# A two-layer diffusion trunk on one core: weight splits on GpSimd, stacked fp32r offset products, and head 0 prepared beside the last recurrence units

## The chip, the cores and the metric

One NeuronCore of a Trainium2 chip runs the whole program once; the metric is the device time of that execution in microseconds. All inputs lie in HBM, and nothing is computed on the host.

## The reference

Two layers with weights of their own each. A layer takes 1152 tokens (128 context tokens and 1024 latent tokens) of width 1024:

```python
h = rmsnorm(x, norm1_g) * (1 + sc1) + sh1            # sc, sh, g: SiLU(cond) @ w_ada + b_ada
q_m, k_m, v_m, o_m, gate_m, conv_in, cq_raw, ckv_raw, krope = split_in(h @ w_in)
y_m = rmsnorm(mlstm_forward + mlstm_backward, mlstm_norm_g) * sigmoid(o_m)   # 4 heads x 64
y_c = silu(layernorm(depthwise_conv31(glu(conv_in)), ln_g, ln_b)) @ pw_w     # 256 channels
q = rmsnorm(rmsnorm(cq_raw) @ w_uq); k, v = rmsnorm_of_keys(rmsnorm(ckv_raw) @ w_ukv, krope)
y_a = softmax(rope(q) @ rope([k, k_ctx]).T / sqrt(96)) @ [v, v_ctx]          # 8 heads
x = x + g1 * (concat(y_m, y_c, y_a) @ w_out)
x = x + g2 * ((silu(gate) * up) @ ffn_w_down)        # gate, up = rmsnorm(x, norm2_g)... @ ffn_w_gu
```

The mLSTM is a matrix memory with an exponential gate, scanned forwards and backwards and stabilised by running maxima. The kernel computes it in tiles of 128 tokens: within a tile as masked scores of keys and queries, between tiles by a carried state.

## The kernel before

Each engine has one hand-written instruction stream, and counted semaphores (`x.at(l, k)`: the k-th signal of layer l) order the streams. An engine executes its own stream strictly in order, so what stands behind a waiting instruction waits too. A Python loop over the two layers writes both, with the same structure.

Products in full precision are made of rounded halves: `a_hi`, `a_lo` and `w_hi`, `w_lo` are fp32r tiles (the value rounded, and what the rounding left), and a product is `a_hi*w_hi + a_lo*w_hi + a_hi*w_lo`. `w_high(n)` (L1199, ScalarE, "ACT" in rows) makes `w_hi` of chunk n, `w_low(n)` (L1588 on VectorE, "DVE") `w_lo`. A second `w_low` on GpSimd ("POOL", L2171) serves the chunks 16 to 23 of `w_out`. Weights for chunk n are double-buffered.

A layer runs in these stages on TensorE ("PE"):

1. Chunks 0 to 12 of `w_in`, 72 matmuls of 384 columns each (`chunk3`, L692), with small work `beside` them: tiles of the gates turned, `ml_tr` and `ml_cols` handed to and fro, key rows (`kr_rows`), `decay` products for `dcol` (L792). On DVE in that time: 31 convolution taps over two channel blocks (`taps`, 62 instructions, L1684, L1686, L1688, L1689), the gate scans, and the nine `w_low(6..14)` between the taps.
2. Chunks 13 to 15 as 72 blocks `dense(first, last)` of three matmuls each (L808 to L810): 24 before the value tiles, 48 spread over the units.
3. `value_tiles` (L768) turn the values; ACT copies them to `vaug` (L1297), which lies where the convolution's input was. So that copy waits for `cv_y`, the end of the taps, and PE waits for the copy.
4. 18 units of the recurrence (`UN`; `for n in range(UN)`): `offsets(n + 2)` (L828), `memory(n)` (L849 to L856), `key_query` (L837), dense blocks and `side(n)`, which holds column sums (L865) and row spreading (L748) for the norms of the latents and of the convolution. `offsets` spreads four rows of gate offsets `rr` over all partitions with fp32 products against a selector `sel` in `mc`.
5. Preparation of attention: head 0's `proj_q` (L962) and `proj_k` (L973), the memory's norm (`hsq`, `hnum`), its turning (L927) and gating (`yt`, `a_hi`, `a_lo`), the convolution's pointwise product (`pointwise`, L941), the turned queries and keys (L980, L986), head 1's projections, 25 products for the row maxima of head 0 (L1003, reduced by DVE at L1980), and `max_rows` (L1011). In layer 0, eight `last_modulation` calls (L718, 128 matmuls of two columns) stand between them. The loads `ctxk`, `krt`, `hw`, `rope_in`, `pw` are issued by SyncE ("SP") once `w_used` has counted 16, the last dense block.
6. Attention: 8 heads of 19 steps (`GLOBAL`), starting with L1024.
7. `w_out` as chunks 16 to 23 (in layer 0, DVE computes 16 modulations beside them, L2063), then the feed-forward part (L1103, L1132).

## Time and profile before

| | |
|---|---|
| time, three runs | 3636.89, 3638.81 (median), 3642.09 us |
| profiled execution | 3644.04 us, its span 3642.2 us |
| mean granted TensorE clock | 0.950 of full speed |
| busy: PE, PEld, DVE, ACT, POOL | 3385.1 (93%), 3020.9, 1878.8 (52%), 864.7 (24%), 321.7 us (9%) |
| layer 0 / layer 1 | the same events about 1795.5 us apart |
| end of the convolution taps on DVE | 272.5 / 2068.1 us |
| PE restarts at the value tiles | 275.43 / 2070.98 us |
| last dense block done | 419.3 / 2214.8 us |
| first attention score (L1024) | 504.75 / 2290.59 us |

Starts are microseconds from the beginning of the span. The four landmarks at the foot of the table cut each layer into the stages that the change touches. The sum in the prediction is made in the profiled execution's time; that execution took 5.2 us longer than the median.

### The profile page before, as it was taken

To read this page: it belongs to the slowest core of one execution; us is meant where nothing else is said; L and a number is where in the kernel's file an instruction comes from. 1 tells how busy PE (TensorE), PEld (TensorE's weight loads), DVE (VectorE), ACT (ScalarE), POOL (GpSimd) and SP (SyncE) were. 2 spreads that over 40 slices of the span, in tenths; PEclk is the share of its full clock that TensorE was granted. 3 is DMA by queue.
4 is the path that set the end of the run, shared out by engine and by line. 5 is a ranking of instruction groups with operands and counts; after the bars stand their busy time and mean duration, and the time that the engine had idled before them with its cause. 6 is when DMAs were issued, how large, how long until landed. Compare 5 with 4: busy or idle time off the path is not lost. (4 is left out here: it accounts for less than half of the span.)

```text
span 3642.2 us, 45449 instructions
## 1 busy us (share of the span) xinstructions
PE 3385.1 (93%) x18642; PEld 3020.9 (83%) x18642; DVE 1878.8 (52%) x3068; ACT 864.7 (24%) x1332; POOL 321.7 (9%) x276
## 2 busy tenths in 40 slices
PE   5989989999899999999989896999997999999998
PEld 4988856557789999999979885655586999999998
DVE  6694644444666556565366655444415434433343
ACT  3212334444221111011132223344422111111100
POOL 0000111222110000000010001122121000000000
PEclk7996879999999999999999888899998999999999
DMA  5210100003322222122021000000110111111111
GB/s 246 88 32 1 62 4 4 3 12 122 106 75 76 86 75 81 63 83 80 28 87 45 18 3 16 2 4 3 45 66 32 50 35 46 35 46 46 46 35 53
DMA packets 44805, 185.60 MB, mean 51 GB/s; under 512 B 5440, under 2 KB 8960, under 8 KB 43136
## 3 DMA queue, kind: packets, MB, share of 16 engines
q1 hardware_dynamic: 37760, 158.58, 12.5%
q0 software_dynamic: 6912, 25.17, 2.4%
q8 instruction: 93, 1.52, 0.2%
q14 instruction: 40, 0.33, 0.0%
HBM read 169.14 MB, written 14.59 MB: 50 GB/s over the span
## 5 line engine op out<-in xcount | busy, mean ns | idle before, releaser
L1103 PE MATMUL ps<-a_hi,gu_hi 128*128 128x384 f32 x2112 | 711.9, 337 | 30.4 <-DVE a_lo L1630 24.2
L1103 PE MATMUL ps<-a_lo,gu_hi 128*128 128x384 f32 x2112 | 710.1, 336 | 0.0
L1103 PE MATMUL ps<-a_hi,gu_lo 128*128 128x384 f32 x2112 | 710.0, 336 | 0.0
L1103 PEld LDWEIGHTS ps<-a_hi,gu_hi 128*128 128x128 f32 x2112 | 400.0, 189 | 36.8 <-issue 18.0
L1103 PEld LDWEIGHTS ps<-a_lo,gu_hi 128*128 128x128 f32 x2112 | 400.1, 189 | 0.0
L1103 PEld LDWEIGHTS ps<-a_hi,gu_lo 128*128 128x128 f32 x2112 | 400.0, 189 | 0.0
L1132 PE MATMUL ps<-g_hi,d_hi 128*128 128x384 f32 x1056 | 354.3, 336 | 4.3 <-DVE g_lo L2081 4.3
L2079 DVE TENSOR_TENSOR at<-ps,sg 128x384 f32<-128x384 f32 x132 | 73.4, 556 | 545.9 <-ACT sg L1511 545.9
L1132 PE MATMUL ps<-g_lo,d_hi 128*128 128x384 f32 x1056 | 354.2, 335 | 0.0
L1132 PE MATMUL ps<-g_hi,d_lo 128*128 128x384 f32 x1056 | 353.9, 335 | 0.0
L1980 DVE TENSOR_REDUCE pmx<-ps 128x1 f32<-128x384 f32 (+1 forms) x400 | 213.4, 543 | 235.5 <-PE ps L1003 235.2
L1038 PE MATMUL ps<-pt,va 128*128 128x512 f32 (+1 forms) x608 | 306.3, 586 | 20.6 <-issue 20.6
L2095 DVE SCALAR_TENSOR_TENSOR z<-ps,mods,z 128x384 f32<-128x384 f32 x352 | 217.7, 618 | 128.0 <-PE ps L1132 128.0
L1511 ACT ACTIVATE sg<-ps 128x384 f32<-128x384 f32 x132 | 65.0, 492 | 906.7 <-PE ps L1103 906.7
L692 PE MATMUL ps<-a_hi,w_hi 128*128 128x384 f32 x1008 | 234.3, 340 | 35.0 <-DVE a_lo L1630 25.1
L1421 ACT ACTIVATE pt<-ps 128x512 f32<-128x512 f32 (+1 forms) x304 | 176.1, 579 | 321.3 <-PE ps L1026 319.4
L1003 PEld LDWEIGHTS ps<-kh,qh 96*128 96x128 f32 x400 | 79.5, 199 | 192.1 <-DVE pmx L1980 187.7
L692 PE MATMUL ps<-a_lo,w_hi 128*128 128x384 f32 x1008 | 230.0, 335 | 0.0
L692 PE MATMUL ps<-a_hi,w_lo 128*128 128x384 f32 x1008 | 229.9, 335 | 0.0
L692 PEld LDWEIGHTS ps<-a_hi,w_hi 128*128 128x128 f32 x1008 | 179.1, 189 | 47.7 <-issue 30.5
L1003 PE MATMUL ps<-kh,qh 96*128 96x384 f32 (+1 forms) x400 | 180.7, 471 | 33.3 <-DVE pmx L1980 29.5
L1132 PEld LDWEIGHTS ps<-g_hi,d_hi 128*128 128x128 f32 x1056 | 199.1, 189 | 5.0 <-DVE g_lo L2081 5.0
(261 smaller groups left out, 5095.2 us busy)
## 6 DMA issues: line engine op xcount, KB each, us to landing
f_raw<-wgu SPq DMA_DIRECT2D x88, 512.0 KB, 4.4
diag<-wada_c POOLq DMA_DIRECT2D x48, 512.0 KB, 3.8
f_raw<-wdn SPq DMA_DIRECT2D x44, 512.0 KB, 4.4
w_raw<-win SPq DMA_DIRECT2D x32, 512.0 KB, 3.6
spill<-z SPq DMA_DIRECT2D x2, 4608.0 KB
z<-spill SPq DMA_DIRECT2D x2, 4608.0 KB, 13.6
w_raw<-wout SPq DMA_DIRECT2D x16, 512.0 KB, 4.0
wada_o<-wada_b SPq DMA_DIRECT2D x16, 512.0 KB, 3.7
```

Of the source, the lines that this page charges most:

```text
L692: mm = MM(ps[:, 3 * (n % 2) + b, 0:BLK], w, a[:, k, b * BLK:(b + 1) * BLK], start=(k == 0 and first), stop=(k == KC - 1 and last))
L1003: MM(ps[:, 5 if h else u % 3, 0:keys.stop - keys.start], qh[h % 2][0:QK, t * P:(t + 1) * P], kh[h % 2][0:QK, keys], start=True, stop=True) ...
L1038: MM(ps[:, bank, 0:n], va[h % 2][:, kt], pt[:, g % 3, 0:n], start=first, stop=(kt == 0 or kt == KTILES - 1)).then_inc(at_pv.sem, 1)
L1103: mm = MM(ps[:, 2 * (v % 2) + part, 0:BLK], w, a[:, k, b * BLK:(b + 1) * BLK], start=(k == 0 and j == 0), stop=(k == KC - 1 and j == 2))
L1132: mm = MM(ps[:, 4 + n % 4, 0:BLK], w[:, f, os_], a[:, f, bs], start=(f == 0 and j == 0), stop=(f == 1 and j == 2))
L1421: A(pt[:, g % 3, 0:n], ps[:, src, 0:n], ACT.Exp, scale=SCALE_A).then_inc(at_exp.sem, 1)
L1511: A(sg[:, v % 2, :], ps[:, 2 * (v % 2), 0:BLK], ACT.Silu).then_inc(f_silu.sem, 1)
L1980: V.tensor_reduce(out, src, AX.X, ALU.max).then_inc(at_mx.sem, 1)
L2079: link(TT(at[:, v % 2, :], ps[:, 2 * (v % 2) + 1, 0:BLK], sg[:, v % 2, :], ALU.mult))
L2095: ins = STT(x[:, o, bs], ps[:, bank, 0:BLK], gate[:, 1:2], x[:, o, bs], ALU.mult, ALU.add)
```

## The change

- `offsets` becomes one product in fp32r over 128 rows instead of an fp32 product over 64: the rounded rows stand in `rrx[0:64]`, what the rounding left in `rrx[64:128]`, and the selector has a one in both halves. For that DVE casts the selector once per layer (L1700), copies `rr` (L1762) and subtracts (L1770), and ACT makes two copies of 64x1152 at chunk 9.
- `w_low(4..15)` goes from DVE to GpSimd, eleven in a row and the last inside the loop of `kw`.
- The six `side_tiles` for key rows run one chunk earlier, the 18 key transposes go inside chunk 12, the copy `dcol` goes from DVE to ACT. Of the 24 dense blocks that stood before the value tiles, 8 stay there or between them (6 before the first value tile that needs the buffers freed by ACT), and 64 are spread over units 0 to 13.
- `proj_q(0)` and `proj_k(0)` run beside units 15 and 16, and their loads are issued once `w_hi(15)` and `w_lo(15)` exist. The order of the sums, means and spreads in `side` is changed, with nine spread rows in one sequence.
- Head 0's preparation: DVE turns the keys, GpSimd the queries; the memory's turning, gating and head 1's projections stand between the maxima of head 0; `pointwise` fills the waits for the turned queries and keys; the low halves of the memory and the convolution are made by GpSimd; the maxima use two PSUM banks instead of three.
- The eight `last_modulation`s are gone from PE; DVE computes 24 modulations instead of 16 beside `w_out` of layer 0.

The core of the diff:

```diff
@@ PE
                     for h in range(HEADS_M):
-                        sel = mc[0:DH, M_SEL + (4 * d + h) * P:M_SEL + (4 * d + h + 1) * P]
-                        mm = MM(ps[:, 3, h * P:(h + 1) * P], sel, rr[:, t * P:(t + 1) * P], start=True, stop=True)
+                        mm = MM(ps[:, 3, h * P:(h + 1) * P], sel[:, (4 * d + h) * P:(4 * d + h + 1) * P], rrx[:, t * P:(t + 1) * P],
+                                start=True, stop=True)
...
-                for k in range(5):
-                    key_tiles(k, 6)
-                    dense(4 * k, 4 * k + 4)
...
                 offsets(0)
-                dense(20, 24)
+                dense(0, 4)
+                pe.wait_ge(ml_dcol.sem, ml_dcol.at(l, 1))
                 for k in range(5):
                     value_tiles(k, 6 + k % 2)
+                    if k < 4:
+                        dense(4 + k, 5 + k)
...
                 for n in range(UN):
                     memory(n)
-                    cuts = [24 + 48 * (2 * n + j) // (2 * UN) for j in range(3)]
+                    cuts = [min(72, 8 + 64 * (2 * n + j) // 28) for j in range(3)]
                     dense(cuts[0], cuts[1])
                     if n + 2 < UN:
                         offsets(n + 2)
-                    if n < 15:
-                        side(n)
+                    side(n)
                     dense(cuts[1], cuts[2])
...
+                    if n == 15:
+                        proj_q(0)
+                    if n == 16:
+                        proj_k(0)
...
-                proj_q(0)
-                last_modulation(0, 2)
-                proj_k(0)
-                last_modulation(2, 4)
-                turned_memory()
-                last_modulation(4, 6)
                 pointwise(0)
-                pe.wait_ge(at_k1.sem, at_k1.at(l, 1))
+                pointwise(1, 0, 1)
                 turn_q(0)
+                pointwise(1, 1, 2)
                 turn_k(0)
-                pointwise(1)
-                proj_q(1)
-                proj_k(1)
+                pointwise(1, 2, NB)
                 for u in range(UNITS):
+                    if u == 2:
+                        turned_memory(0)
+                    if u == 6:
+                        proj_q(1)
+                        turned_memory(1)
+                    if u == 10:
+                        proj_k(1)
                     max_unit(0, u)
+                pe.wait_ge(at_k1.sem, at_k1.at(l, 1))
                 max_rows(0)
@@ DVE
                 dve.wait_ge(z_free_d.sem, z_free_d.at(l, 2))
+                dve.wait_ge(ml_in.sem, ml_in.at(l, 32))
+                V.tensor_copy(sel[:, :], sel_in[:, :])
...
                 taps(9, 13)
-                w_low(11)
+                rows_low()
                 taps(13, 17)
-                w_low(12)
...
-                sums(0)
-                inverse(0)
+                sums(0)
+                inverse(0)
+                keys_turned()
+                hv = den[:, 0, :, :].rearrange("p t h -> p (t h)")
+                dve.wait_ge(ml_hsq.sem, ml_hsq.at(l, 1))
+                link(V.tensor_reduce(hv, hsq[:, :, :], AX.X, ALU.add))
...
                 low_q(0)
+                TT(hn[:, :, :, :], hnum[:, :, :, :], spread(den[:, 2, :, :], DH), ALU.mult).then_inc(ml_h.sem, 1)
                 low_k(0)
...
                 for un in range(UNITS):
+                    if un in (4, 8):
+                        gated_memory(un // 4 - 1)
...
-                        cut = (0, 2, 4, 7, 10, 12, 14, 16)
+                        cut = (0, 3, 6, 10, 14, 18, 21, LATE)
@@ POOL
                 low_halves(0)
+                for n in range(4, 15):
+                    w_low(n)
                 pool.wait_ge(ml_cols.sem, ml_cols.at(l, 6))
...
                 for n in range(UN):
+                    if n == 6:
+                        w_low(15)
@@ SP
+                sp.wait_ge(w_hi_ok.sem, w_hi_ok.at(l, 15))
+                sp.wait_ge(w_lo_ok.sem, w_lo_ok.at(l, 15))
+                sp.dma_start(ctxk[:, :], ctx_ckv[bass.ds(l, 1)].rearrange("a p n -> (a p) n")).then_inc(at_in.sem, 16)
...
                 sp.wait_ge(w_used.sem, w_used.at(l, 16))
```

On DVE, in the convolution of layer 0, the stream before has a weight split after every four taps or so (`x8` are four taps on two channel blocks; `krt` is a copy of key rows, `rb` the last row operation of the gates):

```order
L1739 TENSOR_TENSOR rb<-rr,mrow 64x1152
L1696 COPY krt<-ps 128x32
L1686 SCALAR_TENSOR_TENSOR yc<-u,vecs,yc 128x1182 x4
L1588 TENSOR_TENSOR w_lo<-w_raw,w_hi 128x1024
L1686 SCALAR_TENSOR_TENSOR yc<-u,vecs,yc 128x1182 x8
L1588 TENSOR_TENSOR w_lo<-w_raw,w_hi 128x1024
L1686 SCALAR_TENSOR_TENSOR yc<-u,vecs,yc 128x1182 x8
L1588 TENSOR_TENSOR w_lo<-w_raw,w_hi 128x1024
L1686 SCALAR_TENSOR_TENSOR yc<-u,vecs,yc 128x1182 x8
L1588 TENSOR_TENSOR w_lo<-w_raw,w_hi 128x1024
```

The same place after the change; `rrx` at L1770 is the new subtraction, `rr<-rr` at L1762 the new copy:

```order
L1721 COPY krt<-ps 128x32
L1762 COPY rr<-rr 64x1152
L1763 TENSOR_TENSOR mrow<-mrow 64x9
L1764 TENSOR_TENSOR ra<-ra,mrow 64x1152
L1765 TENSOR_TENSOR rb<-rr,mrow 64x1152
L1711 SCALAR_TENSOR_TENSOR yc<-u,vecs,yc 128x1182 x12
L1770 TENSOR_TENSOR rrx<-rr,lf 64x1152
```

The splits have left DVE, the key rows stand ahead of the row operations, and two operations on 64x1152 are added.

On GpSimd before, from the low halves of the normed input to the products `kw` of the units:

```order
L2177 TENSOR_TENSOR a_lo<-z,a_hi 128x1152 x4
L2188 TENSOR_TENSOR kw<-kt,cols 128x256 x18
L2195 TENSOR_TENSOR rope<-rope_in,vecs 128x288
L2199 TENSOR_TENSOR rope<-rope_in,vecs 128x18x8 x2
L2195 TENSOR_TENSOR rope<-rope_in,vecs 128x320
```

and after:

```order
L2188 TENSOR_TENSOR a_lo<-z,a_hi 128x1152 x4
L2182 TENSOR_TENSOR w_halves<-w_raw,w_halves 128x1024 x11
L2202 TENSOR_TENSOR kw<-kt,cols 128x256 x6
L2182 TENSOR_TENSOR w_halves<-w_raw,w_halves 128x1024
L2202 TENSOR_TENSOR kw<-kt,cols 128x256 x12
L2209 TENSOR_TENSOR rope<-rope_in,vecs 128x288
L2213 TENSOR_TENSOR rope<-rope_in,vecs 128x18x8 x2
```

Twelve splits now stand on GpSimd, eleven of them before its first `kw`, the twelfth behind the sixth.

On PE before, from the last dense block ahead of the value tiles (L768) to unit 0:

```order
L808 MATMUL ps<-a_hi,w_hi 128x384
L809 MATMUL ps<-a_lo,w_hi 128x384
L810 MATMUL ps<-a_hi,w_lo 128x384
L768 MATMUL ps<-cst,z 128x128 x18
L837 MATMUL ps<-z 128x128 x4
L828 MATMUL ps<-rr,mc 128x128 x4
L849 MATMUL ps<-cst_st,z 128x65 x4
L852 MATMUL ps<-vaug,sp_ 128x65 x4
L856 MATMUL ps<-vaug,kw 64x65 x4
L837 MATMUL ps<-z 128x128 x4
```

and after, where L771 are the value tiles and `rrx,sel` the stacked offsets:

```order
L771 MATMUL ps<-cst,z 128x128 x4
L810 MATMUL ps<-a_hi,w_halves 128x384
L811 MATMUL ps<-a_lo,w_halves 128x384
L812 MATMUL ps<-a_hi,w_halves 128x384
L771 MATMUL ps<-cst,z 128x128 x2
L835 MATMUL ps<-z 128x128 x4
L825 MATMUL ps<-rrx,sel 128x128 x4
L847 MATMUL ps<-cst_st,z 128x65 x4
L850 MATMUL ps<-vaug,sp_ 128x65 x4
L854 MATMUL ps<-vaug,kw 64x65 x4
L835 MATMUL ps<-z 128x128 x4
```

The 18 value tiles stood together and have single blocks between them now.

On PE before, from the end of the units to attention in layer 0 (L962 and L973 are head 0's projections, `wada_l` the modulations, L927 the turned memory, L941 the pointwise product, L1003 the maxima):

```order
L962 MATMUL ps<-hw,z 128x96 x18
L718 MATMUL ps<-cond,wada_l 128x2 x16
L973 MATMUL ps<-hw,z 128x128 x9
L973 MATMUL ps<-hw,ctxk 128x128
L718 MATMUL ps<-cond,wada_l 128x2 x16
L927 MATMUL ps<-cst,hnum 128x128 x18
L718 MATMUL ps<-cond,wada_l 128x2 x16
L941 MATMUL ps<-csq,pw 128x384 x6
L980 MATMUL ps<-cst,qk 96x128 x9
L718 MATMUL ps<-cond,wada_l 128x2 x8
L986 MATMUL ps<-cst,qk 96x128 x10
L718 MATMUL ps<-cond,wada_l 128x2 x8
```

and after, from unit 15 on (L909 and L920 are the projections, L889 the pointwise product, L999 and L1005 the turned queries and keys, L1022 the maxima):

```order
L825 MATMUL ps<-rrx,sel 128x128 x4
L909 MATMUL ps<-hw,z 128x96 x18
L847 MATMUL ps<-cst_st,z 128x65 x4
L850 MATMUL ps<-vaug,sp_ 128x65 x4
L854 MATMUL ps<-vaug,kw 64x65 x4
L835 MATMUL ps<-z 128x128 x4
L920 MATMUL ps<-hw,z 128x128 x9
L920 MATMUL ps<-hw,ctxk 128x128
L847 MATMUL ps<-cst_st,z 128x65 x4
L850 MATMUL ps<-vaug,sp_ 128x65 x4
L854 MATMUL ps<-vaug,kw 64x65 x4
L889 MATMUL ps<-csq,pw 128x384 x8
```

Head 0's projections now stand between the last three units, and the pointwise product comes first behind them.

## Rows read from the trace of the kernel before

**Rows 1.** Windows of four stretches (us; busy and count by engine, clock, DMA).

```profile
276.00:323.00 47.00, 46.53 (x240) 39.68 (x239) 13.97 (x38) 10.21 (x24) 1.84 (x3) 0.55 0.00 1
323.00:424.00 101.00, 96.36 (x785) 81.31 (x785) 65.14 (x184) 22.05 (x62) 8.71 (x14) 0.95 0.04 12
424.00:505.00 81.00, 68.27 (x336) 57.11 (x336) 37.97 (x57) 28.77 (x36) 17.03 (x16) 0.67 0.18 58
...
2219.00:2291.00 72.00, 43.98 (x208) 32.97 (x209) 37.90 (x56) 29.23 (x36) 17.65 (x16) 0.74 0.03 9
```

**Rows 2.** Waits of PE, 85 to 280 us (total, times, longest).

```profile
PE ps L768 <- ACT vaug L1297: 12.9, 1, 12.9
PE ps L692 <- DVE w_lo L1588: 5.0, 3, 1.9
```

**Rows 3.** Timeline of the restart (start, duration, count, idle before, releaser).

```profile
275.43 2.49 PE L768 MATMUL ps<-cst,z 128*128 128x128 f32 x10 [12.85 <-ACT vaug L1297]
```

**Rows 4.** Groups of DVE instructions, 137.5 to 273 us.

```profile
L1686 DVE SCALAR_TENSOR_TENSOR yc<-u,vecs,yc 128x1182 f32<-128x1182 f32 x58 | 80.4, 1455 | 0.0
L1588 DVE TENSOR_TENSOR w_lo<-w_raw,w_hi 128x1024 fp32r<-128x1024 f32 x9 | 10.9, 1216 | 0.0
...
L1739 DVE TENSOR_TENSOR rb<-rr,mrow 64x1152 f32<-64x1152 f32 x1 | 1.4, 1351 | 0.0
...
L1696 DVE COPY krt<-ps 128x128 f32<-128x128 f32 (+1 forms) x3 | 0.8, 253 | 12.7 <-PE ps L745 12.7
```

**Rows 5.** Waits of DVE, 1925 to 2070 us.

```profile
DVE krt L1696 <- PE ps L745: 19.8, 2, 13.9
DVE dcol L1822 <- PE ps L792: 6.8, 1, 6.8
```

**Rows 6.** Timeline, 914 to 919 us: DVE beside GpSimd.

```profile
915.41 2.39 POOL L2171 TENSOR_TENSOR w_lo<-w_raw,w_hi 128x1024 fp32r<-128x1024 f32 x1 [11.09 <-ACT w_hi L1199]
...
915.80 3.09 DVE L2063 CUSTOM_DVE_ANT_0 dots_o<-wada_o,crow_o,vecs 128x1024 bf16<-128x1024 f32 x1
...
918.93 1.28 DVE L2063 CUSTOM_DVE_ANT_0 dots_o<-wada_o,crow_o,vecs 128x1024 bf16<-128x1024 f32 x1
```

**Rows 7.** Timeline of PE, full clock: blocks and fp32 offset products.

```profile
386.09 0.34 PE L810 MATMUL ps<-a_hi,w_lo 128*128 128x384 f32 x1
386.27 0.35 PE L808 MATMUL ps<-a_hi,w_hi 128*128 128x384 f32 x1
...
390.28 1.16 PE L828 MATMUL ps<-rr,mc 64*128 64x128 f32 x8
391.37 0.82 PE L748 MATMUL ps<-diag,cst 128*128 128x128 f32 x5
```

**Rows 8.** Timeline of PE, head 1: narrow fp32r products.

```profile
552.80 0.70 PE L1011 MATMUL ps<-ident_r,nmx 128*1 128x128 f32 x9 [0.24 <-DVE nmx L1984]
553.34 1.07 PE L1038 MATMUL ps<-pt,va 128*128 128x512 f32 x2
```

**Rows 9.** Timeline around the preparation, 418 to 506 us.

```profile
419.33 0.49 ACT L1228 ACTIVATE z<-ps 128x384 f32<-128x384 f32 x1 [7.17 <-PE ps L810]
...
477.93 4.16 PE L962 MATMUL ps<-hw,z 128*128 128x96 f32 x36
...
483.17 2.27 PE L973 MATMUL ps<-hw,z 128*128 128x128 f32 x18 [1.08 <-ACTq L1342]
...
504.75 0.76 PE L1024 MATMUL ps<-qh,kh 97*128 97x512 f32 x1 [1.30 <-ACT qh L1412]
```

**Rows 10.** Waits of PE, 2215 to 2292 us.

```profile
PE ps L941 <- DVE a_lo L1949: 13.6, 1, 13.6
```

**Rows 11.** Groups of DVE instructions, 419 to 505 us.

```profile
L1980 DVE TENSOR_REDUCE pmx<-ps 128x1 f32<-128x384 f32 (+1 forms) x25 | 11.7, 539 | 7.2 <-PE ps L1003 7.2
...
L1920 DVE TENSOR_REDUCE small<-sq_ 128x19 f32<-128x1824 f32 x2 | 4.1, 2048 | 6.0 <-ACT sq_ L1356 6.0
...
L1961 DVE MEMSET kh<- 1x1280 f32 x2 | 2.2, 1125 | 0.6 <-issue 0.6
```

More of the change, by code:

```diff
@@ L240, in build @@
         yc = sb("yc", [P, 2, U_LEN], F32, s2)
+        s1 = ExitStack()
+        rr2 = sb("rr2", [P, TOK], F32, s1)
+        rr, rr_raw = rr2[0:DH, :], rr2[DH:P, :]
+        s1.close()
+        rrx = sb("rrx", [P, TOK], F32R, s2)
+        cols = sb("cols", [P, 4, TILES, 8], F32, s2)
+        dcol = sb("dcol", [P, 4, TILES], F32, s2)
+        cst_st = sb("cst_st", [P, 2, 2, 2, DH + 1], F32, s2)
         cx = ExitStack()
@@ new lines, in pointwise @@
+                def pointwise(o, first=0, last=NB):
+                    if o == 0:
+                        pe.wait_ge(ml_out.sem, ml_out.at(l, UN))
+                        pe.wait_ge(cv_act.sem, cv_act.at(l, 1))
+                        pe.wait_ge(pw_in.sem, pw_in.at(l, 32))
+                    elif last == NB:
+                        pe.wait_ge(cv_hi.sem, cv_hi.at(l, 1))
+                    for b in range(first, last):
+                        for c in range(2):
+                            mm = MM(ps[:, 5 - 2 * o + b, 0:BLK], pw[:, c, o, :], csq[:, c, b * BLK:(b + 1) * BLK],
@@ L975, in proj_k, with spread_side, mean_side @@
                         mm.then_inc(at_pk.sem, 1)
+                def spread_side(which, third, free):
+                    pe.wait_ge(free.sem, free.at(l, cv_xc.per if free is cv_xc else 3 * which + third))
+                    if third == 0:
+                        pe.wait_ge(c_diag.sem, c_diag.at(l, which + 1))
+                    side_tiles(7, THIRDS[third], spread_tile, diag, c_row)
+                def mean_side(b):
+                    for c in range(2):
+                        mm = MM(ps[:, 7, 0:BLK], ones, csq[:, c, b * BLK:(b + 1) * BLK], start=(c == 0), stop=(c == 1))
+                    mm.then_inc(cv_mean.sem, 1)
@@ new lines, in _ @@
+                pe.wait_ge(z_free_a.sem, z_free_a.at(l, 10))
+                pe.wait_ge(rr_low.sem, rr_low.at(l, 1))
+                pe.wait_ge(ml_in.sem, ml_in.at(l, 32))
+                offsets(0)
+                dense(0, 4)
+                pe.wait_ge(ml_dcol.sem, ml_dcol.at(l, 1))
+                for k in range(5):
+                    value_tiles(k, 6 + k % 2)
+                    if k < 4:
+                        dense(4 + k, 5 + k)
+                pe.wait_ge(ml_kv.sem, ml_kv.at(l, 10))
@@ L977, in turn_q @@
+                key_query(0).then_inc(ml_pv.sem, 1)
+                offsets(1)
+                pe.wait_ge(ml_c0.sem, ml_c0.at(l, 16))
+                for n in range(UN):
+                    memory(n)
+                    cuts = [min(72, 8 + 64 * (2 * n + j) // 28) for j in range(3)]
+                    dense(cuts[0], cuts[1])
+                    if n + 2 < UN:
+                        offsets(n + 2)
+                    side(n)
+                    dense(cuts[1], cuts[2])
                 def turn_q(h):
@@ L1244, in _ @@
                             act.wait_ge(ml_rows.sem, ml_rows.at(l, 1))
+                            own.link(A(rrx[0:DH, :], rr[:, :], ACT.Copy))
+                            A(rr_up[:, :], rrx[0:DH, :].bitcast(F32), ACT.Copy).then_inc(rr_high.sem, 1)
+                        if n == 10:
+                            act.wait_ge(rr_low.sem, rr_low.at(l, 1))
                         evicted(n, 0)
@@ L1292, in _ @@
                 act.wait_ge(cv_y.sem, cv_y.at(l, 1))
-                exponential(0)
                 for k in range(5):
@@ L1298, in _ @@
                       ACT.Copy).then_inc(ml_kv.sem, 1)
+                exponential(0)
                 for c in range(2):
@@ L1366, in _ @@
+                aa.then_inc(cv_act.sem, 1)
+                act.wait_ge(kr_used.sem, kr_used.at(l, 3))
+                act.wait_ge(at_in.sem, at_in.at(l, 32))
+                first_k(0)
+                square_k(0)
+                for c in range(2):
+                    A(zc(Z_O + c), zc(Z_O + c), ACT.Sigmoid).then_inc(ml_og.sem, 1)
+                nc.scalar.preload_act_table_set("natural_log_exp_and_others")
+                first_root(0)
                 act.wait_ge(ml_num.sem, ml_num.at(l, 1))
@@ L1440, in _ @@
                 pointwise_high(0)
-                act.wait_ge(at_k1.sem, at_k1.at(l, 1))
-                values(0)
+                act.wait_ge(n_var.sem, n_var.at(l, 4))
+                own.link(A(den[:, 1, :, :], den[:, 0, :, :], ACT.Ln))
+                A(den[:, 2, :, :], den[:, 1, :, :], ACT.Exp, scale=-0.5).then_inc(n_root.sem, 1)
                 high_q(0)
```

489 lines of the change are left out of this document (226 added, 263 removed).

## The prediction

> **What bounds the kernel now.** I read the page first, then the windows, then the waits and gaps of PE, and last the timeline around each. PE is busy for 93% of the span, so a gain comes from PE's own work, from its gaps, or from its clock. In each layer the windows [rows 1] set the stretch after 276 us apart: PE is busy for 46.5 of 47 us there, but at a granted clock of 0.55. In the next 101 us it is at 0.95, and the preparation of attention (424 to 505 us in layer 0, 2219 to 2291 us in layer 1) leaves PE 13 and 28 us idle at clocks of 0.67 and 0.74. The rest of the layer is untouched but for `w_out` of layer 0. So the price is set at three places: the stop before the value tiles, the units behind it, and the preparation.
>
> PE's waits before 280 us [rows 2] are three stops for `w_lo` (5.0 us in all, the longest 1.9) and one of 12.9 us for ACT's `vaug`. The timeline [rows 3] has PE restarting at 275.43. ACT had been waiting for the end of the taps at 272.5, so it is DVE that is late.
>
> **Chunks.** Splits on GpSimd wait for nobody's taps in DVE's order, so the two later `w_lo` stops go: 5.0 - 1.9 = 3.1 us in each layer. This moves PE's arrival only, not its restart.
>
> **When the taps end.** DVE's stretch from 137.5 to 273 us [rows 4] has 58 of the taps at 1.39 us each, nine splits (10.9 us) and 12.7 us of idle time for `krt`; the wait for `dcol` is 6.8 us more. In layer 1 the waits are 19.8 and 6.8 us [rows 5]. The key rows come a chunk earlier and `dcol` goes to ACT, so both waits go: 19.5 and 26.6 us. With the splits that is 30.4 and 37.5 us off.
>
> Against it: GpSimd now works beside DVE. In `w_out` of layer 0 [rows 6] a split on GpSimd takes 2.39 us, and the DVE operation that meets it 3.09 instead of 1.28 us: +1.81. Nine meetings cost 16.3 us (none at all would be 0, one whole split each 9 x 2.39 = 21.5). I take the row's value, since the operands are alike. Two operations on 64x1152 come in, at most 1.35 us each [rows 4]: 2.7. The cast of the selector is an estimate of 0.5 in layer 0, and is hidden by a wait in layer 1. There DVE, being earlier, will meet a new wait for key rows; I put it at 4.6 us, between 0 and 9. The taps end 30.4 - 16.3 - 2.7 - 0.5 = 10.9 us earlier in layer 0 and 37.5 - 16.3 - 2.7 - 4.6 = 13.9 in layer 1.
>
> The Trainium skill, "SBUF — State Buffer", section "Who interferes with whom", says that a DVE instruction with two SBUF inputs and a GpSimd instruction that reads SBUF contend, and that whoever comes second is blocked for the whole of the first. The pair of rows agrees: the DVE operation started 0.39 us after the split and ended 3.48 us after that split's start, which is the 2.39 and then 1.09, nearly its own time. By that rule taps laid end to end would each time lose up to the whole split, and the taps would end some 5 us later in each layer than by my sum.
>
> The restart follows the taps closer than before: `vaug`'s eviction stands ahead of `exponential(0)` now. The gap was 275.43 - 272.5 = 2.9 us, of which I take 1.8 off. PE restarts 12.7 us earlier in layer 0 and 15.7 in layer 1.
>
> **Dense blocks.** 18 blocks that filled the time before the wait now stand behind it. A block is three matmuls 0.17 to 0.18 us apart (the first two of [rows 7]): 18 x 0.52 = 9.4 us, **added** behind the restart. PE therefore arrives some 12.5 us (3.1 + 9.4) earlier at the wait, which stays about as long as it was (12.3 us in layer 0, 9 in layer 1) although the taps end earlier.
>
> **Offsets.** At full clock the eight fp32 passes of one unit take 1.09 us to the next instruction (the last two of [rows 7]); some 0.19 of that is the hand-over, which stays. Four fp32r products cost between 4 x 0.06 = 0.24 (nine narrow ones in 0.54 us [rows 8]) and 0.45 (if each is as long as one fp32 pass of two); I take 0.35, nearer to the middle as each has a new selector to load. 17 of 18 stand behind the restart: 17 x (0.90 - 0.35) = 9.4 us off; by the bounds 7.7 to 11.2.
>
> **Head 0's projections.** 36 and 18 records [rows 9] take 4.16 and 2.27 us: 6.5 us more in the units, and 1.5 us for the units 14 to 17, which have no dense blocks left to cover the round through DVE and ACT (0 to 5). The same 6.5 us leave the preparation, where they are counted below.
>
> **Clock.** From 276 us on PE spent about 0.9 x 47 + 0.1 x 101 = 52 us at the lower of its two levels. The units now hold 64 blocks of dense work instead of 48, all before unit 14, so more of each unit is steady product. The fall itself follows the stop, which stays. I guess that 32 us stay low: 20 us less, at half the speed, give back about 9.4 us. This is the least certain term: 0 if the low stretch is as long as now, 25 if the clock never falls.
>
> End of the units: layer 0 -12.7 + 9.4 - 9.4 + 6.5 + 1.5 - 9.4 = **-14.1**; layer 1 **-17.1** by its earlier restart.
>
> **Preparation.** From the last block to the first score it is 504.75 - 419.3 = 85.5 us [rows 9], in layer 1 75.8; the 10 us between them are the `last_modulation`s, which are gone. In layer 1 PE's longest wait is 13.6 us for `a_lo` [rows 10], the end of a chain through the memory's norm, turning and gating that all stood before the pointwise product. Now the pointwise product waits for nothing of it. I laid the new streams against each other with the durations of the rows, from the end of the last `memory`: DVE is done with the unit at 3.1, `sums(0)` (2.05 [rows 11]) at 5.4, the inverse at 7.8, the keys turned at 12.2 beside GpSimd's queries, the reduction of `hsq` at 15.0, `low_q` at 18.4, `hn` at 21.0, `low_k` at 22.7, the constants (two memsets at 1.13 [rows 11] and what goes with them) at 27.1. Then the 25 maxima: 25 x 0.54 = 13.5 us [rows 11], `sums(1)`, the inverse and the gating 5.5, and head 1's projections on PE between them, 6.4 us [rows 9], since two banks let PE run ahead only by one. That is 52.8, and 2.8 us for `max_rows` and the copy as before: **55.6 us**. Off: 29.9 in layer 0, 20.2 in layer 1.
>
> **`w_out` of layer 0.** DVE has 24 modulations beside six chunks where it had 16. Chunks of four modulations leave no idle time, so PE waits at the end for about 1.5 us (0 to 4).
>
> **Sum:** -14.1 - 17.1 - 29.9 - 20.2 + 1.5 = -79.8 us. 3644.0 - 79.8 = 3564.2 us in the profiled execution's terms; the median lies 5.2 lower, 3559 us. I say 3560.
>
> **Rivals.**
> 1. Contention eats what DVE gains: each of the nine splits meets a tap on either side, 3.2 us each and not 1.8, and the restart is 12 us later per layer than in the sum. For it speaks [rows 6], against it that GpSimd is idle between splits. 3560 + 24 = 3584. Chance 0.12.
> 2. The clock: with more dense work the low stretch nearly disappears and gives the remaining 15 us back in each layer, 3532; chance 0.12. That it stays as long as now gives 3560 + 19 = 3579; chance 0.08.
> 3. The preparation stays serial: DVE's chain carries `keys_turned`, `low_q`, `hn` and `low_k` one after the other, and GpSimd's share runs beside them at the price of [rows 6] again. 10 us more per layer: 3580. Chance 0.08.
> 4. The stacked offsets are no cheaper than before, each product bound by loading its selector: +9.4 x 2, 3579. Chance 0.03, and it fits the row of 0.06 us badly.
> 5. Slower than before: the taps hold the shared path and a split on GpSimd lands late. PE works 72 matmuls at 0.17 to 0.18 us on a chunk [rows 7], 12.5 us; a split that starts within 1 us of `w_hi` has some 10 us of slack. Only if every tap in a row wins, so that a split waits for seven taps (10 us), does it stop PE; at 14 us late, eleven chunks in two layers would cost 22 x 4 = 88 us and undo all: 3560 + 88 = 3648. The row of 2.39 us speaks against it. Chance 0.02.
>
> The forecast itself has 0.55. It, 1, 2 (both sides), 3 and 4 lie between 3532 and 3584; with the bounds of the unknown terms (offsets 3, `w_out` 3, new waits 5) I reach from 3530 to 3590 for 8 in 10. A change of 0.2% (7 us) is about what a measurement here can tell from none. Faster by more than that in all cases but the last and an unforeseen one: 0.96; within 0.2%: 0.01; slower: 0.03.
>
> **What would show it.** PE's waits have no `w_lo` stop behind the first, and restarts near 263 and 2055 us after a stop of 12 and 9 us. DVE's taps stretch has no idle time for `krt` or `dcol` in layer 0, its taps mean over 1.6 us where GpSimd runs. Four offset products take 0.35 us. The last block lies about 14 and 17 us earlier; the windows behind the restart have a clock of 0.55 for some 30 us only. The first score comes 56 us after the last unit. I would be wrong above all if the clock behaved otherwise, or if one of the new streams in the preparation waited for another in a circle that I did not see: the first score more than 65 us after the last unit would be that.

## The result and the profile after

The changed kernel takes 3606.49 us in the median of four runs (3604.86 to 3610.51), the kernel before 3638.88: the ratio is 0.9912 with a 95% interval from 0.9895 to 0.9929. It is faster, as forecast, but by 32 us and not by 79. The profiled execution has a span of 3602.6 us (3642.2 before) and a mean clock of 0.951 (0.950). A "tap" below is one instruction of the convolution on VectorE, a "split" one `w_low`.

PE's and GpSimd's timeline where the stop for `vaug` stood before ([rows 3]), with the starts and durations in microseconds and in brackets the idle time before and its releaser:

```profile
193.60 12.23 POOL L2182 TENSOR_TENSOR w_halves<-w_raw,w_halves 128x1024 fp32r<-128x1024 f32 x1 [9.83 <-ACT w_halves L1211]
...
205.89 0.79 PE L691 MATMUL ps<-a_hi,w_halves 128*128 128x384 f32 x3 [1.12 <-POOL w_halves L2182]
...
206.08 3.23 POOL L2182 TENSOR_TENSOR w_halves<-w_raw,w_halves 128x1024 fp32r<-128x1024 f32 x1 [0.25 <-ACT w_halves L1211]
...
220.90 42.00 POOL L2182 TENSOR_TENSOR w_halves<-w_raw,w_halves 128x1024 fp32r<-128x1024 f32 x2 [11.59 <-ACT w_halves L1211]
...
260.62 1.33 PE L691 MATMUL ps<-a_hi,w_halves 128*128 128x384 f32 x3 [28.37 <-POOL w_halves L2182]
```

GpSimd's split that starts at 220.90 runs together with the next in one row of 42.00 us, 39.67 of them its own; alone a split took 2.39 ([rows 6]). The time that a split waits for its data path counts in its duration. PE idles 28.37 us for it, ahead of chunk 12 and not ahead of the value tiles. The split at 193.60 lasts 12.23 us and is just in time: PE loses 1.12 us. DVE's timeline over the same time shows what GpSimd was waiting for:

```profile
203.65 3.41 DVE L1770 TENSOR_TENSOR rrx<-rr,lf 64x1152 fp32r<-64x1152 f32 x1
207.09 48.36 DVE L1711 SCALAR_TENSOR_TENSOR yc<-u,vecs,yc 128x1182 f32<-128x1182 f32 x34
255.38 0.33 DVE L1713 SCALAR_TENSOR_TENSOR csq<-u,vecs,yc 128x128 f32<-128x128 f32 x1
...
257.10 1.27 DVE L1714 SCALAR_TENSOR_TENSOR csq<-u,vecs,yc 128x1024 f32<-128x1024 f32 x1
258.58 0.09 DVE L1834 MEMSET vaug<- 128x36 f32 x1 [0.21 <-DVE csq L1714]
```

34 taps stand in one row from 207.09 to 255.4 us. The first of them was blocked by the split of 206.08; alone in its window it reads:

```profile
207.09 3.47 DVE L1711 SCALAR_TENSOR_TENSOR yc<-u,vecs,yc 128x1182 f32<-128x1182 f32 x1
```

That is 2.0 us more than the 1.44 of its kind, and (48.36 - 2.0) / 34 = 1.36 us are left for each, as fast as before (1.39 in [rows 4]): the others lost nothing to the waiting split. When the last instruction of the taps has ended at 258.4 the waiting split runs and PE restarts 2.2 us later. In layer 1 the same stop is 27.6 us long.

The windows that answer to [rows 1], with the stop as the first:

```profile
232.00:260.00 28.00, 0.25 (x3) 0.01 (x1) 26.45 (x23) 2.12 (x6) 28.00 (x1) 0.56 0.00 0
...
285.00:332.00 47.00, 45.85 (x316) 40.14 (x315) 22.22 (x62) 11.86 (x33) 2.46 (x4) 0.82 0.02 6
332.00:427.00 95.00, 92.61 (x741) 84.59 (x740) 55.35 (x159) 30.86 (x73) 13.20 (x19) 0.87 0.04 11
427.00:482.00 55.00, 37.54 (x152) 25.47 (x153) 39.32 (x61) 22.83 (x28) 14.00 (x11) 0.72 0.01 4
```

PE is busy for 0.25 us of 28 in the stop (the first column behind the length); GpSimd (the fifth) counts as busy for all of it, as its split waits. The units run at a clock of 0.82 and then 0.87, where it was 0.55 and then 0.95. The preparation has shrunk to 55 us. For its order, the timeline of the preparation (answers to [rows 9] and [rows 11]):

```profile
426.80 6.96 PE L889 MATMUL ps<-csq,pw 128*128 128x384 f32 x16 [1.25 <-DVE ni L1870]
...
438.61 2.16 PE L999 MATMUL ps<-cst,qk 128*96 128x128 f32 x9 [4.84 <-POOL qk L2280]
...
444.26 2.54 DVE L2004 TENSOR_TENSOR hn<-hnum,den 128x2304 f32<-128x2304 f32 x1
...
447.09 1.55 DVE L1970 SCALAR_TENSOR_TENSOR kl<-ps,vecs,kh 96x1280 fp32r<-96x1280 f32 x1 [0.28 <-ACT kh L1429]
...
451.28 1.12 DVE L2010 MEMSET kh<- 1x1280 f32 x1 [0.30 <-issue]
```

and, at its end:

```profile
481.86 0.76 PE L1043 MATMUL ps<-qh,kh 97*128 97x512 f32 x1 [1.30 <-ACT qh L1433]
```

The pointwise product (L889) starts 1.3 us after the units, `hn` follows at 444.26 and the last constant starts at 451.28; the first score stands at 481.86.

Three measures per layer serve from here on. They are read from the timeline: PE's stop; the units, from the first to the last product with `kw`; and the preparation, from there to the first score. "Low" is how much of the units lay at the lower of the two clock levels. Two layers of one kernel do the same work, so their difference gives the price of a low microsecond: (140.0 - 135.5) / (50.5 - 41.0) = 0.47 us in the changed kernel, 3.8 / 7.8 = 0.49 in e1. The next column takes 0.48 us for each low microsecond off the units, which leaves their length at full clock.

| kernel | time, us | ratio (95%) | stop, us | units, us (low) | the same at full clock, us | preparation, us |
|---|---|---|---|---|---|---|
| before | 3638.9 | | 12.9 / 12.9 | 133.4 (44.9) / 133.4 (44.8) | 111.8 / 111.9 | 87.4 / 77.8 |
| changed | 3606.5 | 0.9912 (0.9895 to 0.9929) | 28.4 / 27.6 | 135.5 (41.0) / 140.0 (50.5) | 115.8 / 115.8 | 56.5 / 57.2 |
| e1 | 3562.7 | 0.9778 (0.9761 to 0.9794) | 12.3 / 12.3 | 132.4 (34.1) / 136.2 (41.9) | 116.0 / 116.1 | 56.5 / 56.6 |
| e2 | 3578.8 | 0.9821 (0.9804 to 0.9839) | 17.5 / 14.2 | 139.4 (49.4) / 136.5 (43.2) | 115.7 / 115.8 | 57.5 / 57.6 |
| e3 | 3712.8 | 1.0183 (1.0164 to 1.0202) | 32.3 + 16.0, twice | | | |
| e4 | 3568.4 | 0.9797 (0.9775 to 0.9819) | 12.3 / 12.3 | 136.4 (42.8) / 133.9 (37.5) | 115.9 / 115.9 | 57.5 / 56.5 |
| e5 | 3596.0 | 0.9859 (0.9839 to 0.9880) | 11.7 / 11.7 | 149.3 (44.4) / 152.6 (51.2) | 128.0 / 128.0 | 56.7 / 56.5 |
| e6 | 3553.5 | 0.9747 (0.9729 to 0.9766) | 3.9 / 3.9 | 132.0 (51.2) / 129.2 (45.2) | 107.4 / 107.5 | 57.4 / 56.6 |
| e7 | 3587.1 | 0.9842 (0.9826 to 0.9859) | 12.3 / 12.3 | 133.9 (48.5) / 133.2 (45.9) | 110.6 / 111.2 | 71.8 / 71.1 |
| e8 | 3561.6 | 0.9775 (0.9759 to 0.9792) | 8.0 / 8.0 | 136.1 (42.3) / 139.8 (49.4) | 115.8 / 116.1 | 57.4 / 57.4 |
| e9 | 3550.2 | 0.9749 (0.9733 to 0.9765) | 0.6 / 0.6 | 132.4 (52.3) / 130.7 (47.5) | 107.3 / 107.9 | 57.4 / 57.5 |
| e10 | 3569.1 | 0.9807 (0.9791 to 0.9824) | 10.9 / 10.1 | 134.0 (37.5) / 136.4 (42.9) | 116.0 / 115.8 | 57.2 / 57.5 |

At full clock every kernel with the same work in its units comes out within 0.4 us of the others in both layers (115.7 to 116.1 for the changed kernel, e1, e2, e4, e8 and e10), so the column can be read as work, and the rest of a unit stage as clock.

Ratios are to the kernel before on the same chip, whose median there was 3643.2 to 3644.0 us for e1 to e10, so compare ratios. In the row e9, stops, units and preparation are from e9b, the same kernel run again. Points of time early in layer 0 carry 4 us that no edit makes: the first tap starts at 137.75 us in the kernel before, at 140.21 in the changed kernel, at 140.16 in e1, and between 136.6 and 141.1 in the rest, as more or fewer microseconds before 106 us are at the lower clock.

### The profile page after: what moved, and what is told of

It is laid out like the page before. It is cut to its first block and busy times, and to the rows that moved or that the text cites. A ratio compares the mean times of both kernels' runs of the same rounds, so it can differ in the third digit from the quotient of the medians.

```text
span 3602.6 us, 44990 instructions
## 1 busy us (share of the span) xinstructions
PE 3326.2 (92%) x18370; PEld 2979.8 (83%) x18370; DVE 1900.5 (53%) x3087; ACT 873.7 (24%) x1346; POOL 496.5 (14%) x306
## 5 line engine op out<-in xcount | busy, mean ns | idle before, releaser
L691 PE MATMUL ps<-a_hi,w_halves 128*128 128x384 f32 x2016 | 422.6, 341 | 85.1 <-POOL w_halves L2182 57.1
L691 PEld LDWEIGHTS ps<-a_hi,w_halves 128*128 128x128 f32 x2016 | 359.3, 191 | 97.6 <-POOL w_halves L2182 57.8
L2182 POOL TENSOR_TENSOR w_halves<-w_raw,w_halves 128x1024 fp32r<-128x1024 f32 x40 | 204.2, 5107 | 398.8 <-ACT w_halves L1211 398.8
L1022 PEld LDWEIGHTS ps<-kh,qh 96*128 96x128 f32 x400 | 77.9, 196 | 200.8 <-DVE pmx L1978 198.9
L691 PE MATMUL ps<-a_lo,w_halves 128*128 128x384 f32 x1008 | 232.9, 339 | 0.0
L1022 PE MATMUL ps<-kh,qh 96*128 96x384 f32 (+1 forms) x400 | 182.4, 463 | 40.2 <-DVE pmx L1978 39.8
```

Source lines behind the costliest of these rows:

```text
L691: mm = MM(ps[:, 3 * (n % 2) + b, 0:BLK], w, a[:, k, b * BLK:(b + 1) * BLK], start=(k == 0 and first), stop=(k == KC - 1 and last))
L1022: MM(ps[:, 5 if h else 6 + u % 2, 0:keys.stop - keys.start], qh[h % 2][0:QK, t * P:(t + 1) * P], kh[h % 2][0:QK, keys], start=True, stop=T ...
L2182: G.tensor_tensor(w_lo[:, n % 2, :], w_raw[:, n % 2, :], w_hi[:, n % 2, :].bitcast(F32), ALU.subtract).then_inc(w_lo_ok.sem, 1)
```

## The experiments

**e1: the splits back on VectorE.** Nothing else of the change is undone.

```diff
@@ POOL
-                for n in range(4, 15):
-                    w_low(n)
@@ DVE, and so on for 4 to 15
                 taps(7, 10)
+                w_low(10)
                 taps(10, 13)
                 rows_low()
                 taps(13, 14)
+                w_low(11)
                 taps(14, 18)
+                w_low(12)
```

> The changed kernel with all weight splits back on VectorE between the taps (4 to 15), everything else as changed. Theory A (starvation): the 28 us stop before chunk 12 was a split on GpSimd that could not start while taps ran end to end; without it PE reaches the value tiles near 250 us, restarts near 259 us (284 in the changed kernel), and the same in layer 1: 3606 - 2 x 25 = 3556 us, between 3545 and 3567. Theory C (the shortfall is in the units, which hold 64 dense blocks and lose their clock): the stop only moves to vaug and the units get longer, 3590 to 3606 us.

3562.66 us, ratio 0.9778. The timeline of its DVE:

```profile
207.10 1.22 DVE L1613 TENSOR_TENSOR w_halves<-w_raw,w_halves 128x1024 fp32r<-128x1024 f32 x1
208.23 10.97 DVE L1713 SCALAR_TENSOR_TENSOR yc<-u,vecs,yc 128x1182 f32<-128x1182 f32 x8
219.11 1.23 DVE L1613 TENSOR_TENSOR w_halves<-w_raw,w_halves 128x1024 fp32r<-128x1024 f32 x1
...
232.09 1.23 DVE L1613 TENSOR_TENSOR w_halves<-w_raw,w_halves 128x1024 fp32r<-128x1024 f32 x1 [0.86 <-ACT w_halves L1211]
...
247.19 1.23 DVE L1613 TENSOR_TENSOR w_halves<-w_raw,w_halves 128x1024 fp32r<-128x1024 f32 x1 [2.98 <-ACT w_halves L1211]
...
260.93 1.28 DVE L1716 SCALAR_TENSOR_TENSOR csq<-u,vecs,yc 128x1024 f32<-128x1024 f32 x1
```

A split costs VectorE 1.1 us between the taps, and three times VectorE waits for ScalarE's high half (0.86 and 2.98 us here, and 1.41 us ahead of the split at 180.57). PE's only long stop is the old one, 12.25 us for `vaug` in each layer, and PE restarts at 262.96 us in layer 0; I had expected some 259. Theory A holds, and theory C, that the shortfall was in the units, has at most the few microseconds by which their rows in the table differ.

**e2: GpSimd keeps the splits, VectorE drains once in four taps.** `settle(1)` lets a tap start when the instruction before the last has ended, so two overlap a little; `settle(0)` waits for the last one. That wait is the drain.

```diff
-                            own.settle(1)
+                            own.settle(0 if k % 2 and c == 0 else 1)
```

> The changed kernel, splits on GpSimd; the taps drain the engine once in four instructions (the wait is for the instruction just before, not the one before that). Theory A: GpSimd gets in at each drain, so no split lasts over about 8 us and the stop of 28 us falls under 3 us; each of nine splits costs VectorE 1.8 to 2.4 us, the drains 16 x 0.1 us: 3560 to 3575 us. Theory B (contention shares the path instruction by instruction, and GpSimd is just slower): a drain changes nothing, 3606 us.

3578.81 us, ratio 0.9821: 4 us slower than the expected range, but far from theory B's 3606. GpSimd's timeline:

```profile
191.60 2.50 POOL L2182 TENSOR_TENSOR w_halves<-w_raw,w_halves 128x1024 fp32r<-128x1024 f32 x1 [10.21 <-ACT w_halves L1211]
204.09 3.18 POOL L2182 TENSOR_TENSOR w_halves<-w_raw,w_halves 128x1024 fp32r<-128x1024 f32 x1 [9.98 <-ACT w_halves L1211]
217.50 3.02 POOL L2182 TENSOR_TENSOR w_halves<-w_raw,w_halves 128x1024 fp32r<-128x1024 f32 x1 [10.24 <-ACT w_halves L1211]
230.51 3.28 POOL L2182 TENSOR_TENSOR w_halves<-w_raw,w_halves 128x1024 fp32r<-128x1024 f32 x1 [9.99 <-ACT w_halves L1211]
245.61 2.81 POOL L2182 TENSOR_TENSOR w_halves<-w_raw,w_halves 128x1024 fp32r<-128x1024 f32 x1 [11.82 <-ACT w_halves L1211]
```

No split of the taps' stretch lasts over 3.4 us in either layer, and no stop for a split is left. The price is on VectorE: the taps end later, and the stop for `vaug` is 17.5 and 14.2 us.

**e3: the kernel before with nothing changed but its splits 4 to 15 on GpSimd.**

```diff
@@ DVE
-                w_low(4)    ... and so on to 15
@@ POOL
                 low_halves(0)
+                for n in range(4, 15):
+                    w_low(n)
```

> The kernel before with only the splits 4 to 15 moved to GpSimd. Theory A: splits wait for the end of each unbroken row of taps, PE stops for w_lo by some 10 to 30 us in each layer; some of it is hidden since dcol's wait breaks the row and the restart waits for the taps anyway: 3650 to 3690 us. Theory B: contention of 1.8 us per split against 1.1 us of VectorE's own: 3640 to 3650 us.

3712.78 us, ratio 1.0183: 69 us slower than the kernel before, more than the expected 3650 to 3690, since the stop for a split does not take the place of the stop for `vaug` but stands beside it. The first stands in PE's and GpSimd's timeline:

```profile
192.40 45.86 POOL L2158 TENSOR_TENSOR w_lo<-w_raw,w_hi 128x1024 fp32r<-128x1024 f32 x2 [9.59 <-ACT w_hi L1199]
...
235.99 1.33 PE L692 MATMUL ps<-a_hi,w_hi 128*128 128x384 f32 x3 [32.29 <-POOL w_lo L2158]
```

and PE's, later:

```profile
310.54 2.49 PE L768 MATMUL ps<-cst,z 128*128 128x128 f32 x10 [15.95 <-ACT vaug L1297]
```

Two splits take 45.86 us (the first 43.53), PE idles 32.29 us for the first of them and then 15.95 for `vaug`. In layer 1 the two stops have the same lengths. When the first split was issued, no tap was running yet, but the last row operation of the gates:

```profile
191.47 1.35 DVE L1737 TENSOR_TENSOR rb<-rr,mrow 64x1152 f32<-64x1152 f32 x1
```

The taps start at 192.85, behind it and a short copy, and the split waits for the whole row of them, in both layers. So this one part of the change alone costs 69 us, and the other parts gain far more than the total shows.

**e4: splits 4 to 10 on GpSimd, 11 to 15 on VectorE.** The first split on VectorE waits for the load of the next weights as well, which orders the two engines' signals.

> The changed kernel with the splits 4 to 10 on GpSimd and 11 to 15 on VectorE. Theory A: only the rows of 12 and 34 taps starve GpSimd; split 10 still meets the row of 12 taps (12 us, which the buffer just covers), the later ones are safe: 3553 to 3568 us, at most 5 us from the kernel with all splits on VectorE. Theory C: 3590 to 3606 us.

3568.44 us, ratio 0.9797, 0.4 us outside the expected range and 5.8 above e1, with an interval that overlaps e1's. The split 10 lasts 12.26 us in the row of 12 taps here too, and PE loses 1.16 us to it. So of the rows of taps in the changed kernel it is the last, of 34, that does the harm.

**e5: e1 with fp32 offsets.** The result misses the low parts of the rows.

```diff
-                        mm = MM(ps[:, 3, h * P:(h + 1) * P], sel[:, ...], rrx[:, t * P:(t + 1) * P],
+                        mm = MM(ps[:, 3, h * P:(h + 1) * P], sel[0:DH, ...].bitcast(F32), rrx[0:DH, t * P:(t + 1) * P].bitcast(F32),
```

> The kernel with the splits on VectorE (e1), its offsets again fp32 products over 64 rows, of the rounded rows only, so the low parts are left out of the result. Prices the offsets term: I have 0.55 us a unit at full clock, 9.4 us a layer, so 3562.7 + 19 = 3582 us and the units 9 to 11 us longer in each layer. Rival 4 of the prediction (no cheaper): 3563 us.

3595.98 us: 33 us more than e1 (30 by the ratios), not 19. The four products of one unit in the changed kernel, at full clock, to the start of the next line:

```profile
387.76 0.56 PE L825 MATMUL ps<-rrx,sel 128*128 128x128 f32 x4
388.15 0.43 PE L749 MATMUL ps<-diag,cst 128*128 128x128 f32 x2
```

0.39 us, where [rows 7] had 1.09: 0.70 a unit, 11.9 us a layer. In the prediction I had left 0.19 of the 1.09 standing as a hand-over; it goes too. At full clock the units are 12.0 us longer than in e1, as that says. The rest of the 16.9 and 16.4 us by which they are longer is clock: 10.3 and 9.3 us more of them are low.

**e6: e1 with 24 dense blocks ahead of and between the value tiles, 48 in the units.**

```diff
-                dense(0, 4)
+                dense(0, 20)
...
-                        dense(4 + k, 5 + k)
+                        dense(20 + k, 21 + k)
...
-                    cuts = [min(72, 8 + 64 * (2 * n + j) // 28) for j in range(3)]
+                    cuts = [24 + 24 * (2 * n + j) // 16 if n < 8 else min(72, 48 + 24 * (2 * n - 16 + j) // 12) for j in range(3)]
```

> e1 with 24 dense blocks ahead of and between the value tiles and 48 in the units (24 in units 0 to 7, 24 in 8 to 13), as many as the kernel before had. The stop for vaug is 12.25 us in e1 and would cover 16 more blocks (8.3 us) for nothing. If the units are bound by PE's work: 3 to 4 us of stop left and 8.3 us off each layer, 3546 us. If the units with fewer blocks are bound by the round through VectorE and ScalarE, or lose more of their clock, the gain goes there: 3555 to 3565 us, with new gaps ahead of the memory products.

ScalarE's order changes with it: it copies two of the three slices of chunk 13 ahead of `vaug`, the third in unit 2.

3553.51 us, ratio 0.9747: 9 us less than e1 (11 by the ratios), not 17. The stop shrinks by 8.3 us in each layer, and at full clock the units are 8.6 us shorter, so the work is off the path as it should be. But 17.1 and 3.3 us more of them are low, which takes 8.2 and 1.6 us back.

**e7: e1 with head 0's projections behind the units.**

> e1 with head 0's projections behind the units instead of beside units 15 and 16. My sum had +6.5 +1.5 us for them in the units. If the preparation is the chain on ScalarE and VectorE that I laid out, then the projections now come first in it and everything behind waits for their results: preparation 8 to 10 us longer, units 6.5 shorter (or less, where the units 15 to 17 wait for VectorE anyway): 3566 to 3575 us. If the projections were of no use beside the units: 3563 us or less.

3587.11 us, ratio 0.9842: 24 us slower than e1, more than expected. The preparation is 15.3 and 14.5 us longer. The units are 5.4 and 4.9 us shorter at full clock, but with 14.4 and 4.0 us more of them low they are 1.5 longer and 3.0 shorter as they ran. Each of the two projections starts a chain on ScalarE and VectorE; that beside the units this chain is hidden fits the longer preparation, and was not tested by itself.

**e8: e1 with the split of chunk 14 behind the taps.**

> e1 with the split of chunk 14 taken from between the taps and put behind unit 0 on VectorE. If the end of the taps sets PE's restart to the microsecond, the restart is 1.1 us earlier in each layer and the time 2 us less, 3560.5 us, which the runs may not separate but the trace will; if something else holds the restart, the gap ahead of the value tiles stays 12.25 us.

3561.60 us, not to be told from e1. The trace tells more: the stop is 8.0 us instead of 12.25, which is 4.2 off and not 1.1. The 2.98 us that VectorE had waited for the high half (e1's row at 247.19) go with the split's own 1.1. The units have the same length as e1's at full clock and take back 3.7 and 3.6 us with 8.2 and 7.5 us more of them low.

**e9: e6 with the splits 9, 13 and 14 where the high half is ready.**

```diff
-                w_low(9)
                 row_offsets()
+                w_low(9)
...
-                taps(18, 22)
+                taps(18, 23)
                 w_low(13)
-                taps(22, 26)
+                taps(23, 28)
                 w_low(14)
-                taps(26, CONV_WIDTH)
+                taps(28, CONV_WIDTH)
```

> The kernel with splits on VectorE and 24 dense blocks ahead of the stop (e6), with the splits 9, 13 and 14 put two to eight instructions later, behind the row offsets and behind taps 23 and 28, where ScalarE has already delivered the high half (VectorE had waited 1.4, 0.9 and 3.0 us for it). If VectorE's end of the taps sets the restart, the stop of 3.9 us goes and PE's own work sets it: 3.9 us off each layer, 3553.5 - 8 = 3546 us, with no stop over 1 us. If the restart is set by something else, 3553 us.

Its median is 3550.16 us and its ratio 0.9749, the same as e6's within the intervals; 3546 were expected. The one execution of it that was profiled took 13478.77 us, for a reason that is not known, and is left out of the ratio. The same kernel was run again for its profile:

> The same kernel as e9_splits_when_ready, for its profile. If the end of the taps set the restart, the stop for vaug is under 1 us (3.9 in e6) and the time 3550 us; if not, a stop of 3.9 us stands there.

3549.73 us. The timeline has the stop at 0.6 us in both layers, 3.3 us less than in e6; e9's median is 3.4 us lower, which the intervals do not separate. There is no stop left ahead of the units here, and yet 52.3 and 47.5 us of the units are low, more than the 44.9 and 44.8 of the kernel before with its stop of 12.9. So the clock falls in the units without a stop ahead of them too.

**e10: the changed kernel with one drain in the last 34 taps.**

```diff
-                            own.settle(1)
+                            own.settle(0 if k == 20 and c == 0 else 1)
```

> The changed kernel, splits on GpSimd, with one single drain among the last 34 taps (ahead of tap 20, near 226 us in layer 0). Theory A (GpSimd gets in only at a gap, then holds the path for its whole instruction): the split issued near 221 us ends near 228.5 us instead of 260 us, so PE's stop of 28 us ahead of that chunk goes; the next split, issued near 234 us, has no drain left and waits for the end of the taps, and PE stops for it ahead of the dense blocks, some 12 to 16 us. 3606 - 2 x 12 = 3582 us. Theory B (a steady share): one drain is worth 0.1 us, 3606 us and the stop of 28 us stays.

3569.12 us, ratio 0.9807: 37 us off the changed kernel, for one wait in each layer, and 13 below the 3582 expected. GpSimd's timeline, and DVE's around the drain:

```profile
218.87 9.62 POOL L2182 TENSOR_TENSOR w_halves<-w_raw,w_halves 128x1024 fp32r<-128x1024 f32 x1 [11.59 <-ACT w_halves L1211]
231.87 2.83 POOL L2182 TENSOR_TENSOR w_halves<-w_raw,w_halves 128x1024 fp32r<-128x1024 f32 x1 [3.39 <-ACT w_halves L1211]
246.97 15.89 POOL L2182 TENSOR_TENSOR w_halves<-w_raw,w_halves 128x1024 fp32r<-128x1024 f32 x1 [12.26 <-ACT w_halves L1211]
```

```profile
226.26 3.47 DVE L1711 SCALAR_TENSOR_TENSOR yc<-u,vecs,yc 128x1182 f32<-128x1182 f32 x1
```

The split of 218.87 ends at 228.49, behind the drain at 226.26. The expected stop for the next one does not come: it is issued at 231.87 and runs at the next change of taps with no drain there, in 2.83 us. The split after it, at 246.97, waits for the end of the taps again (15.89 us) but PE does not need it yet. No stop for a split over 1.1 us is left in either layer, and the gain is larger than expected. So one drain opened the way for more than its own moment.

## Why the prediction was wrong

The sum was 79.8 us in the profiled execution's terms and the spans differ by 39.6. Laid out by the three measures, the missing 40.2 us are these. The units begin 18.6 us later than forecast in layer 0 (289.8 against 283.9 - 12.7) and 13.0 in layer 1 (2055.3 against 2079.5 less layer 0's measured gain of 22.9 at the first score, less 15.7, with the 1.5 of `w_out` added). Some 2.5 of the 18.6 us were lost before the first tap, to the clock (140.21 against 137.75). They last 3.5 and 8.0 us longer than the forecast of 133.4 - 1.4 = 132.0. The preparation is 1.0 and 0.4 us shorter than the 57.5 and 57.6 that the forecast gives on this measure. That is 41.7, and 1.5 us come back behind the last first score.

- **Chunks: this step failed.** "Splits on GpSimd wait for nobody's taps in DVE's order" is true of the order of instructions and false of the path to the data. A long row of taps shut GpSimd out, and the stop of 3.1 us that was to go became one of 28. e3 shows the cost alone, e1, e2 and e10 each take it away in another way. It was rival 5, which I gave 2 in 100 on the strength of [rows 6], where GpSimd came first. Its mechanism was right (every tap in a row wins), its shape was not: I let every split be late by the same amount, and it was one long row that held one split for 40 us.
- **When the taps end.** I charged VectorE 16.3 us for nine meetings. In layer 0 only six of its instructions were lengthened, by 11.9 us together (1.8 to 2.2 each), one by each of the first six splits there; the seventh waited for the end of the taps and met none. The taps ended at 258.4 us, 3.2 us before my 261.6. The Trainium skill, "SBUF — State Buffer", section "Who interferes with whom", by which the second is blocked for the whole of the first, gave 5 us later for the same sum. Where a tap is blocked the trace agrees with it (3.47 us at 207.09 for a tap of 1.44, behind a split that ended at 209.31). For a split that comes second it does not: blocked for the whole of one tap, the split of 220.90 would have gone in within 1.4 us, and it was kept out for 37.3, through 29 changes of taps. The size of a meeting was nearly right (2.0 us and not 1.8); what the sum lacked is that the split can be the one that waits, and for a whole row.
- **The restart.** With the splits back on VectorE it came at 262.96 (forecast 262.7), with a stop of 12.25 us (12.3). The agreement is in part luck. e1 has nine splits on VectorE (10.9 us) and three waits for ScalarE's high half (5.2 us, 3 of them taken away again in e8), where the sum had 16.3 us of meetings; and e1 reached its first tap 2.4 us later than the kernel before, by the clock. The 12.3 was also not the sum's own: 12.85 + 12.5 - 12.7 is 12.65.
- **Offsets: too small.** 11.9 us a layer and not 9.4; rival 4 fell.
- **Dense blocks: right, 16 of the 18 lie in the units** (8.3 us; e6 gives 8.6).
- **Head 0's projections: about right.** From the kernel before to e1 the units grow by 4.2 us at full clock: 8.3 for the blocks, -11.9 for the offsets, and 7.8 for the rest, where I had 6.5 + 1.5. Taken out again alone (e7) they give 5.4 and 4.9 us, so 2.4 and 2.9 of the 7.8 are something else in the units, which no run names.
- **Clock: the term was wrong, and so was its reason.** The price of a low microsecond was half one, as I used it. Of the 20 low microseconds that were to go, 11 and 3 went in e1, and in the changed kernel 4 went in layer 0 and 6 came on top in layer 1: 9.4 us forecast, 5.2 and 1.4 measured in e1, 1.9 and -2.7 in the changed kernel. I had the fall follow the stop; e9 has no stop, and 52.3 and 47.5 us low. Equal work in the units goes with 34 to 50 low microseconds, so the number of dense blocks does not fix it either (48 blocks: 45 to 52). What does stays open. The changed kernel's long stop may have a part in its 41 and 50 us, but e8, without it, has 42 and 49.
- **Preparation: right** (though its terms add up to 52.5 where the sum has 52.8). Laid out from the end of the units at 425.1 us, `hn` was forecast to be done at 21.0 and ended at 21.7 (446.80), the constants at 27.1 and 28.1, the first score at 55.6 and 56.8.
- **`w_out` of layer 0:** no cost. From the first score to PE's wait at the second norm it is 479.4 us, before 479.9.

With the one step undone, the sum comes out: e1's span is 82.0 us below that of the kernel before, the forecast was 79.8. It does so as a sum of terms that err both ways, and that is luck as well. The units of e1 are 4.6 us longer than forecast in the two layers together, since the clock gave 12.2 us less than I had and the offsets 5 us more. Against that the preparation is 2.0 us shorter than forecast, layer 1's units begin 2.4 us earlier (2018.35 against 2079.45 - 44.5 - 15.7 + 1.5), and 2.5 us are gained behind the last first score.

## What to carry to other kernels

Before moving an elementwise operation to GpSimd, look at what VectorE does over the time in which the result is due: a long unbroken row of two-operand instructions held GpSimd off for all its length here (37 and 41 us), and a pair of rows taken where VectorE has gaps does not show it. If the work must stay on GpSimd, a drain on VectorE just after it becomes ready let it in (e10), though with one drain in the row a later split still waited 15.9 us; moving it back cost 1.1 us a piece here and was the better trade. And a wait that ends up on the critical engine is worth a rival with a shape, not only a price: ask for the longest row, not for the mean.
